# A four-layer transformer block and a three-branch block on one core: two-head attention groups, traded operand pairs, and a mixer tail in another order

## The chip, the cores and the metric

One core of a Trainium2 chip runs the whole program. The metric is the device time of one execution in microseconds; the page also gives the span, from the first to the last instruction of the core. A matmul runs on TensorE (PE), its weight load is listed as PEld; VectorE is DVE, ScalarE is ACT, GpSimd is POOL and the queue engine is SP.

## What is computed

T = 256 tokens of width 1024 pass through four layers and then a second block. A layer is: half a feed-forward, a mixer, half a feed-forward, and a gated addition of a projected per-layer embedding (the phase called `ple`):

```python
for layer in range(DEPTH):                    # 4
    h = x + 0.5 * swiglu(rmsnorm(x, g[0]), w_ffn_gu[layer, 0], w_ffn_down[layer, 0])
    h = h + mixer(rmsnorm(h, g[1]))           # hgrn2, mlstm, sliding window, hgrn2
    h = h + 0.5 * swiglu(rmsnorm(h, g[2]), w_ffn_gu[layer, 1], w_ffn_down[layer, 1])
    gate = jax.nn.sigmoid(rmsnorm(h, g[3]) @ w_ple_gate[layer])
    x = h + gate * (p[layer] @ w_ple_proj[layer])
```

The hgrn2 mixer ends with a norm per head, a gate and a projection:

```python
    o = rmsnorm(from_chunks(o), g_norm)
    o = o.reshape(B, T, D_MODEL).astype(x.dtype) * jax.nn.silu(og)
    return o @ w_out
```

The second block has three branches: dilated window attention (three groups of 8 heads of width 64, strides 1, 4 and 16, mixed by a softmax over their log-denominators, which is the same as one softmax over all three groups' masked scores), grouped attention with rotary positions (8 heads of 64, 2 key heads), and attention to 256 memory tokens (4 heads of 128). Each branch is gated by a silu and projected, the three are merged by sigmoid gates, projected once more, normalised and added to x. All inputs and outputs are float32.

## The kernel before

Activations lie feature-major in SBUF, as 8 chunks of 128 features by 256 tokens. Every weight matrix is cut into 407 **units** of 1 MB (128 partitions by 2048 numbers). A unit n passes through four engines:

- SP loads it into one of 4 slots of `raw`, as soon as unit n-4 has been split.
- ACT (`high`, L1127) rounds it to the 32-bit matmul type: `w_hi` = cast(raw), into one of 3 slots, once PE has used unit n-3.
- DVE (`low`, L1526) takes the rest: `w_lo` = raw - w_hi. It counts up `weights_split`.
- PE multiplies it: 48 matmuls of 128x128 by 128x256, three for each product of a block (`act_hi` by `w_hi`, `act_hi` by `w_lo`, `act_lo` by `w_hi`). `project` (L641) does 8 chunks k of a column unit, `project_tokens` (L656) the same with tokens on the partitions, `rows` (L670) a row unit into four accumulating banks.

Activations are split in the same way: `xg_hi`/`xg_lo` hold the normalised input of a phase without the norm's factor, and `mo_hi`/`mo_lo` the middle operand (hidden values of the feed-forward, the mixer's output, the embedding p in slots 4 and 5). DVE writes `xg` for the next phase in `next_operand` (two chunks: two TENSOR_SCALAR at L1568, then two SCALAR_TENSOR_TENSOR at L1571) and counts `x_updated` and `xg_ready`; the next phase's first `project` waits for `xg_ready` chunk by chunk. The norm's factor follows behind: ACT squares x (L1132), DVE adds the 8 chunks of squares (a TENSOR_REDUCE over a strided view, L1540), PE sums over partitions by a matmul with ones (`norm_sums`, L688; in the second block L685), ACT takes the logarithm and the exponential (L1138, L1141) into `rstd`, and DVE multiplies it into each PSUM bank as it is read (`scale`, L1577). Each engine has one instruction stream written out by hand. No scheduler reorders it, so what stands ahead on an engine is waited for.

The phases that the change touches:

- **ple** (units n0 to n0+4): PE does `rows(n0)` on p, then four `project`s of the gate weights, with `norm_sums` behind the first. DVE scales bank u, ACT takes its sigmoid (L1186), and DVE (`gated(u)`, L1648 and L1649) multiplies and adds to chunks 2u and 2u+1 of x. `xg` is still read by the last `project`, so the first `next_operand` waits for `weights_used` n0+5, which is that project's end.
- **hg** (hgrn2 mixer, layers 0 and 3): while PE does the projections n0+14 and n0+15, it also makes the outputs of the heads (L802 to L804) into banks 4 to 7 and the sums of their squares (`both_sums`, L813) into banks 2 and 3. ACT takes logarithms (L1247) and exponentials (L1253) of two pairs at a time. DVE normalises (L1812) and multiplies the gate (L1815); ACT casts (`operand`, L1257), DVE subtracts (`low_part`, L1819), and the output projection `w_out` starts as the pairs come (`mo_ready`).
- **second**: the memory operand is made during the last ple, with its own square sum on DVE (L1665). PE then does two memory projections, waits for the two norms (L1023, L685, L1028), and goes on. The attention runs in three stages, between the projections of other units: 9 units with the memory and grouped attention (6 **wide** groups of 4 slots by 256 keys, one in flight), 9 units with the first four dilated heads of each group (8 **narrow** groups: one head, 128 queries, 512 masked keys, two in flight), and 6 gate units with the last four heads (8 narrow groups, two in a unit). In each unit PE does: `project`, `rotate` (L1063, for the rotary products, stages one and two), `values(u-1)` (L931), `turn(u)` (transposes, L920), `scores(u+1)` (L910). DVE does: `scale`, `rope` (L2133 to L2136), `take(u-1)` (L1989), `logits(u+1)` (mask L1967, maximum L1969, bias L1970), `low`, `probs(u+1)` (L1978, L1981). ACT does:

```python
                    exps(0)
                    for u in range(9):
                        copies(u)
                        exps(u + 1)
                        high(n0 + 10 + 9 * half + u + SPLIT)
```

where `exps` (L1335) waits for the bias and `copies` (L1344) for the transposes.

## Time and profile before

| | |
|---|---|
| three runs | 2711.62, 2709.26, 2704.3 us, median 2709.26 us |
| the profiled execution | 2703.97 us |
| its span | 2702.2 us, mean granted TensorE clock 0.990 |
| PE | 2602.0 us busy (96%), 21152 matmuls |
| DVE | 1766.9 us (65%) |
| ACT | 1211.0 us (45%) |
| DMA | 435.51 MB, queue of the weights busy 44.3% |
| chain that ended last | PE 80%, DVE 13%, ACT 5%, issue 2% |

The matmuls overlap in the array: each is listed with about 283 ns, while one starts every 0.12 us. So the count times 0.12 us tells how long a unit keeps PE, 48 of them 5.76 us, and a unit that lasts longer has waited. An idle time is listed with what ended it.

### The profile page before, as it was taken

The page shows a single profiled execution, that of the slowest core. Times are in us where ns is not written, and L with a number is a line of the kernel's source. Part 1 is how long each engine was busy: PE and PEld are TensorE (multiplying, and loading weights), DVE is VectorE, ACT ScalarE, POOL GpSimd, SP SyncE. Part 2 cuts the span into 40 slices and gives each one's busy share as a digit, 9 for nine tenths or more (in the row PEclk, how much of TensorE's full clock was granted, in tenths as well). Part 3 has the DMA queues.
Part 4 walks back from the last instruction along what each step waited for, and adds up shares of the span by engine and source line. Part 5 has one row for each costly group of instructions (what it writes and reads, how often), then busy time and mean ns, then how long its engine had stood idle before and what let it go on. Part 6 is the DMA issues. An engine that isn't in the chain of part 4 may idle for free.

```text
span 2702.2 us, 49646 instructions
## 1 busy us (share of the span) xinstructions
PE 2602.0 (96%) x21152; PEld 2543.3 (94%) x21152; DVE 1766.9 (65%) x2230; ACT 1211.0 (45%) x1279; POOL 5.2 (0%) x13
## 2 busy tenths in 40 slices
PE   8999999999999999999969999999999999999997
PEld 8999999999998999999959999999999998888897
DVE  6558675586565755865676558656856568666665
ACT  4444354444444544444464335434354445433543
POOL 0000000000000000000000000000000000000000
PEclk9999999999999999999999999999999999999999
DMA  7554245445542455455424544544435544333351
GB/s 268 182 186 172 79 157 191 186 156 188 187 171 98 177 198 183 160 187 182 164 93 140 189 177 156 192 180 156 156 107 195 187 171 156 125 125 111 109 181 69
DMA packets 60193, 435.51 MB, mean 161 GB/s; under 512 B 6720, under 2 KB 6848, under 8 KB 7552
## 3 DMA queue, kind: packets, MB, share of 16 engines
q1 hardware_dynamic: 59184, 429.05, 44.3%
q0 software_dynamic: 848, 4.06, 0.4%
q8 instruction: 131, 2.15, 0.3%
q14 instruction: 30, 0.25, 0.0%
HBM read 432.04 MB, written 1.05 MB: 160 GB/s over the span
## 4 chain that ended last, share of the span: by engine, by line
PE 80%; DVE 13%; ACT 5%; issue 2%; DMA 0%; ACTq 0%; DVEq 0%
PE ps L641 52%; PE ps L670 19%; PE ps L656 4%; DVE w_lo L1526 4%; ACT w_hi L1127 3%; PE ps L780 2%; DVE xg_lo L1571 1%; DVE xg_hi L1568 1%; DVE scratch L1577 1%; DVE x L1633 1%; DVE tiny L1969 0%; PE ps L910 0%; DVE scratch L1981 0%; ACT scratch L1335 0%; DVE scratch L2085 0%
## 5 line engine op out<-in xcount | busy, mean ns | idle before, releaser
L1526 DVE TENSOR_TENSOR w_lo<-raw,w_hi 128x2048 fp32r<-128x2048 f32 x407 | 932.2, 2291 | 544.6 <-ACT w_hi L1127 544.3
L641 PE MATMUL ps<-xg_hi,w_hi 128*128 128x256 f32 x4240 | 1211.7, 286 | 27.7 <-DVE xg_lo L1571 24.8
L641 PE MATMUL ps<-xg_hi,w_lo 128*128 128x256 f32 x4240 | 1200.4, 283 | 0.0
L641 PE MATMUL ps<-xg_lo,w_hi 128*128 128x256 f32 x4240 | 1200.2, 283 | 0.0
L1127 ACT CAST w_hi<-raw 128x2048 fp32r<-128x2048 f32 x407 | 771.5, 1896 | 475.1 <-PE ps L670 250.9
L641 PEld LDWEIGHTS ps<-xg_hi,w_hi 128*128 128x128 f32 x4240 | 813.9, 192 | 37.8 <-issue 20.7
L641 PEld LDWEIGHTS ps<-xg_hi,w_lo 128*128 128x128 f32 x4240 | 814.2, 192 | 1.1 <-issue 0.5
L641 PEld LDWEIGHTS ps<-xg_lo,w_hi 128*128 128x128 f32 x4240 | 814.1, 192 | 0.0
L670 PE MATMUL ps<-mo_hi,w_hi 128*128 128x256 f32 x1568 | 445.0, 284 | 4.8 <-DVE xg_hi L1568 3.6
L670 PE MATMUL ps<-mo_hi,w_lo 128*128 128x256 f32 x1568 | 443.7, 283 | 0.0
L670 PE MATMUL ps<-mo_lo,w_hi 128*128 128x256 f32 x1568 | 443.7, 283 | 0.0
L1156 ACT ACTIVATE scratch<-scratch 128x256 f32<-128x256 f32 x176 | 73.7, 419 | 582.9 <-DVE scratch L1598 582.8
L670 PEld LDWEIGHTS ps<-mo_hi,w_hi 128*128 128x128 f32 x1568 | 300.9, 192 | 7.4 <-DVE xg_hi L1568 6.1
L670 PEld LDWEIGHTS ps<-mo_hi,w_lo 128*128 128x128 f32 x1568 | 301.0, 192 | 0.0
L670 PEld LDWEIGHTS ps<-mo_lo,w_hi 128*128 128x128 f32 x1568 | 301.0, 192 | 0.0
L1598 DVE TENSOR_TENSOR scratch<-ps,rstd 128x256 f32<-128x256 f32 x176 | 74.5, 423 | 145.8 <-PE ps L641 126.3
L641 PE MATMUL ps<-mo_hi,w_hi 128*128 128x256 f32 x352 | 102.5, 291 | 11.8 <-DVE mo_lo L1819 8.9
L641 PE MATMUL ps<-mo_hi,w_lo 128*128 128x256 f32 x352 | 101.3, 288 | 0.0
L641 PE MATMUL ps<-mo_lo,w_hi 128*128 128x256 f32 x352 | 101.2, 287 | 0.0
L1602 DVE TENSOR_TENSOR scratch<-scratch 128x256 f32<-128x256 f32 x176 | 75.2, 427 | 37.6 <-ACT scratch L1156 37.1
L656 PE MATMUL ps<-w_hi,xg_hi 128*128 128x256 f32 x320 | 91.7, 287 | 0.0
L656 PE MATMUL ps<-w_hi,xg_lo 128*128 128x256 f32 x320 | 90.6, 283 | 0.0
(273 smaller groups left out, 2175.2 us busy)
## 6 DMA issues: line engine op xcount, KB each, us to landing
raw<-weights_dram SPq DMA_DIRECT2D x407, 1024.0 KB, 4.8
x<-x_t_dram SPq DMA_DIRECT2D x1, 1024.0 KB, 7.7
scratch<-c_second_dram POOLq DMA_DIRECT2D x1, 1024.0 KB, 12.1
scratch<-p_t_dram POOLq DMA_DIRECT2D x4, 256.0 KB, 3.8
scratch<-mem_t_dram POOLq DMA_DIRECT2D x1, 1024.0 KB, 7.6
out_dram<-x SPq DMA_DIRECT2D x2, 512.0 KB, 2.6
common<-c_common_dram POOLq DMA_DIRECT2D x1, 640.0 KB, 9.1
smalls<-smalls_dram SPq DMA_DIRECT2D x1, 152.0 KB, 4.9
```

Source lines behind the costliest of these rows:

```text
L641: last = nc.tensor.matmul(bank(e, ring)[:, half * T:(half + 1) * T], l, r, start=(k == 0 and j == 0 and half == 0), stop=(k == KC - 1 and ...
L656: last = nc.tensor.matmul(bank(e, ring)[:, b * T:(b + 1) * T], l, r, start=(k == 0 and j == 0), stop=(k == KC - 1 and j == 2))
L670: last = nc.tensor.matmul(ps[:, 4 + c // 2, (c % 2) * T:(c % 2 + 1) * T], l, r, start=(first and k == 0 and j == 0 and c % 2 == 0), stop=( ...
L780: last = nc.tensor.matmul(o, HG_SUFFIX[:, at_:at_ + keys], upper(HG_PQ[:, at_:at_ + P], w), start=True, stop=True)
L1127: nc.scalar.copy(w_hi[:, m % SPLIT, :], raw[:, m % RAW, :]).then_inc(weights_hi, 1)
L1156: nc.scalar.activation(FFN_T[:, 2 + j % 2], FFN_T[:, j % 2], ACT.Silu).then_inc(silu_ready, 1)
L1526: V.tensor_tensor(w_lo[:, m % SPLIT, :], raw[:, m % RAW, :], w_hi[:, m % SPLIT, :].bitcast(F32), ALU.subtract).then_inc(weights_split, 1)
L1568: V.tensor_scalar(xg_hi[:, c], x[:, c], gain(g, c), None, ALU.mult).then_inc(x_updated, 1)
L1571: V.scalar_tensor_tensor(xg_lo[:, c], x[:, c], gain(g, c), xg_hi[:, c].bitcast(F32), ALU.mult, ALU.subtract).then_inc(xg_ready, 1)
L1577: V.tensor_tensor(dst, pair(e % ring, True), row(rstd[:], 2), ALU.mult).then_inc(bank_read, 1)
L1598: V.tensor_tensor(FFN_T[:, j % 2], pair(e)[:, 0], rstd[:], ALU.mult).then_inc(up_scaled, 1)
L1602: V.tensor_tensor(FFN_H[:, j % 2], FFN_T[:, 2 + j % 2], FFN_T[:, 4 + j % 2], ALU.mult).then_inc(hidden_value, 1)
```

## The change

It has seven parts.

1. **Trading pairs.** The two operand pairs are now called `left` and `right`, and `operands(i)` says which is xg and which mo in phase i: they trade places behind each of the first three ple phases. In ple, the next input is then written to the pair that is free, so the wait for `weights_used` n0+5 goes and `next_operand` moves ahead: two chunks at u = 1, 2 and 3 each, the last two behind `gated(3)`. At u = 3 ACT takes the sigmoid first and casts the weights second. The phase before the second block doesn't trade, but its memory operand moves by one u.
2. **Square sums.** `sum_chunks` replaces the TENSOR_REDUCE of all 17 norms and of the memory: three TENSOR_TENSOR adds, of 1024, 512 and 256 columns, each waiting for the one before.
3. **norm_sums in ple** is issued inside the first `project`, ahead of its chunk 4, and no longer behind it.
4. **The tail of hg.** ACT takes four logarithms, then four exponentials; the cast of unit n0+17 moves from between them to behind `operand(2)`. DVE scales gate 2 ahead of the first normalisation, and takes the low part of unit n0+17 last. PE makes the second half of the sums two chunks earlier.
5. **Two-head groups.** A dilated group now holds two heads (2 slots by 512 keys), with both heads' matmuls alternating; there are 4 groups in a stage and one in flight, in the same buffers and banks as the wide groups. Group u belongs to unit u, so the later units of a stage have none.
6. **values** of every group go through blocks first and heads second.
7. **Weights first.** In all three stages ACT's `high` stands ahead of `copies` and `exps` of the unit; in the third stage DVE's `low` stands ahead of `logits`.

```diff
+        def operands(i):
+            trades = min(sum(k == "ple" for k, _ in phases[:i]), DEPTH - 1)
+            return (right, left) if trades % 2 else (left, right)
...
-            for h in range(4):
+            for hp in range(2):
                 for n in range(TB):
-                    r = head_half(h)
-                    g = dict(slots=1, width=512, k0=0, scale=HD ** -0.5, scores=[], values=[], h=h, n=n)
+                    g = dict(slots=2, width=512, k0=0, scale=HD ** -0.5, scores=[], values=[], masked=True, hp=hp, n=n)
                     own_block = slice(n * P, (n + 1) * P)
                     for a, col, keys in ((0, 0, slice(0, T)), (1, 256, own_block), (2, 384, own_block)):
-                        c = 2 * a + h // 2
-                        g["scores"].append((col, keys.stop - keys.start, QA[r, c, own_block], KA[r, c, keys]))
+                        for h in range(2):
+                            r, c = head_half(h), 2 * a + hp
+                            g["scores"].append((512 * h + col, keys.stop - keys.start, QA[r, c, own_block], KA[r, c, keys]))
...
-                project(n0 + 1, e0, XG, (xg_ready, x0))
-                norm_sums(i)
+                project(n0 + 1, e0, XG, (xg_ready, x0), besides={4: lambda: norm_sums(i)})
...
-                project(n0 + 15, e0 + 15, XG, ring=2, besides={2: lambda: both_sums(2)})
+                project(n0 + 15, e0 + 15, XG, ring=2, besides={0: lambda: both_sums(2)})
...
-                    for r, col, vs in groups[g]["values"]:
-                        for j, (v, block_) in enumerate(vs):
+                    heads = groups[g]["values"]
+                    blocks = len(heads[0][2])
+                    for j in range(blocks):
+                        for r, col, vs in heads:
+                            v, block_ = vs[j]
...
-                roots(0)
-                high(n0 + 14 + SPLIT)
-                roots(2)
-                gate(2)
+                roots()
                 operand(0)
                 operand(1)
+                gate(2)
                 gate(3)
                 operand(2)
+                high(n0 + 14 + SPLIT)
                 operand(3)
...
                     for u in range(9):
+                        high(n0 + 10 + 9 * half + u + SPLIT)
                         copies(u)
                         exps(u + 1)
-                        high(n0 + 10 + 9 * half + u + SPLIT)
...
+            def sum_chunks(v, out):
+                link(V.tensor_tensor(v[:, 0:4], v[:, 0:4], v[:, 4:8], ALU.add))
+                link(V.tensor_tensor(v[:, 0:2], v[:, 0:2], v[:, 2:4], ALU.add))
+                return V.tensor_tensor(out, v[:, 0], v[:, 1], ALU.add)
...
-                V.tensor_reduce(SQ_SUM, SQ.rearrange("p c t -> p t c"), AX_X, ALU.add).then_inc(square_sum, 1)
+                sum_chunks(SQ, SQ_SUM).then_inc(square_sum, 1)
...
                 for u in range(4):
-                    if u == 3:
-                        gated(2)
-                        dve.wait_ge(weights_used, n0 + 5)
-                        if not to_second:
-                            next_operand(i, 0, 2)
                     scale(n0 + 1 + u, e0 + u, PLE_T[:, 2 * u:2 * u + 2])
-                    if u in (1, 2):
-                        gated(u - 1)
-                    if u < 2 or (u == 2 and to_second):
+                    if u and not to_second:
+                        next_operand(i, 2 * (u - 1), 2)
+                    if 0 < u < 3 and to_second:
+                        memory_operand(i, 2 + 2 * u, 2)
+                    if u < 3:
                         low(n0 + 1 + u + SPLIT)
+                    gated(u)
...
                 for u in range(6):
                     scale(n0 + 28 + u, e0 + 28 + u, t, ring=2)
-                    for g in (2 * u, 2 * u + 1):
-                        take(g - 2)
-                        logits(g + 2)
+                    take(u - 1)
+                    low(n0 + 28 + u + SPLIT)
+                    logits(u + 1)
                     dve.wait_ge(m["gate"], u + 1)
                     V.tensor_tensor(SE_O[:, c:c + 2], SE_O[:, c:c + 2], t, ALU.mult).then_inc(m["gated"], 1)
-                    low(n0 + 28 + u + SPLIT)
-                    probs(2 * u + 2)
-                    probs(2 * u + 3)
+                    probs(u + 1)
```

**DVE at the end of the first ple.** L1526 (now L1504) is `low`, L1577 (L1563) `scale`, L1648 and L1649 (L1634, L1635) `gated`, L1568 and L1571 (L1554, L1557) `next_operand`. Before, from u = 2 on:

```order
L1577 TENSOR_TENSOR scratch<-ps,rstd 128x512
L1648 TENSOR_TENSOR scratch<-scratch,ps 128x512
L1649 TENSOR_TENSOR x<-x,scratch 128x512
L1648 TENSOR_TENSOR scratch<-scratch,ps 128x512
L1649 TENSOR_TENSOR x<-x,scratch 128x512
L1568 TENSOR_SCALAR xg_hi<-x,smalls 128x256 x2
L1571 SCALAR_TENSOR_TENSOR xg_lo<-x,smalls,xg_hi 128x256 x2
L1577 TENSOR_TENSOR scratch<-ps,rstd 128x512
L1568 TENSOR_SCALAR xg_hi<-x,smalls 128x256 x2
L1571 SCALAR_TENSOR_TENSOR xg_lo<-x,smalls,xg_hi 128x256 x2
```

Now, from u = 2 on:

```order
L1563 TENSOR_TENSOR scratch<-ps,rstd 128x512
L1554 TENSOR_SCALAR right_hi<-x,smalls 128x256 x2
L1557 SCALAR_TENSOR_TENSOR right_lo<-x,smalls,right_hi 128x256 x2
L1504 TENSOR_TENSOR w_lo<-raw,w_hi 128x2048
L1634 TENSOR_TENSOR scratch<-scratch,ps 128x512
L1635 TENSOR_TENSOR x<-x,scratch 128x512
L1563 TENSOR_TENSOR scratch<-ps,rstd 128x512
L1554 TENSOR_SCALAR right_hi<-x,smalls 128x256 x2
L1557 SCALAR_TENSOR_TENSOR right_lo<-x,smalls,right_hi 128x256 x2
L1634 TENSOR_TENSOR scratch<-scratch,ps 128x512
L1635 TENSOR_TENSOR x<-x,scratch 128x512
```

The first operand chunks now stand ahead of the last `scale` by a whole unit; only chunks 6 and 7 stay behind the last `gated`.

**ACT at the tail of the first hg.** L1247 (now L1231) is the logarithm, L1253 (L1237) the exponential, L1242 (L1226) the silu of a gate, L1257 (L1241) the operand's cast, L1127 (L1108) `high`. Before:

```order
L1247 ACT_TABLE_LOAD
L1247 ACTIVATE scratch<-ps,eps 128x512 x2
L1253 ACT_TABLE_LOAD
L1253 ACTIVATE scratch<-scratch 128x512 x2
L1127 CAST w_hi<-raw 128x2048
L1247 ACT_TABLE_LOAD
L1247 ACTIVATE scratch<-ps,eps 128x512 x2
L1253 ACT_TABLE_LOAD
L1253 ACTIVATE scratch<-scratch 128x512 x2
L1242 ACT_TABLE_LOAD
L1242 ACTIVATE scratch<-scratch 128x512
L1257 CAST mo_hi<-scratch 128x512 x2
```

Now:

```order
L1231 ACT_TABLE_LOAD
L1231 ACTIVATE scratch<-ps,eps 128x512 x4
L1237 ACT_TABLE_LOAD
L1237 ACTIVATE scratch<-scratch 128x512 x4
L1241 CAST right_hi<-scratch 128x512 x2
L1226 ACT_TABLE_LOAD
L1226 ACTIVATE scratch<-scratch 128x512 x2
L1241 CAST right_hi<-scratch 128x512
L1108 CAST w_hi<-raw 128x2048
L1241 CAST right_hi<-scratch 128x512
```

Two table loads, one cast of weights and one silu are gone from ahead of the first operand casts.

**ACT in the second attention stage**, where L1335 (now L1315) is `exps` and L1344 (L1324) `copies`. Before, a stretch of three units:

```order
L1335 ACTIVATE scratch,tiny<-scratch,tiny 128x512
L1127 CAST w_hi<-raw 128x2048
L1344 COPY scratch<-ps 128x512
L1335 ACTIVATE scratch,tiny<-scratch,tiny 128x512
L1127 CAST w_hi<-raw 128x2048
L1344 COPY scratch<-ps 128x512
```

Now:

```order
L1315 ACTIVATE scratch,tiny<-scratch,tiny 128x512 x2
L1108 CAST w_hi<-raw 128x2048
L1324 COPY scratch<-ps 128x1024
L1315 ACTIVATE scratch,tiny<-scratch,tiny 128x512 x2
L1108 CAST w_hi<-raw 128x2048
L1324 COPY scratch<-ps 128x1024
```

The rows follow one another alike, but the cast now belongs to the unit of the copy behind it, not to the unit of the exponentials ahead of it. In unit u it waits only for that unit's `project`.

## Rows read from the trace of the kernel before

**Rows 1.** The page, part 1: busy time of each engine.
```profile
PE 2602.0 (96%) x21152; PEld 2543.3 (94%) x21152; DVE 1766.9 (65%) x2230; ACT 1211.0 (45%) x1279; POOL 5.2 (0%) x13
```
**Rows 2.** Waits of PE: us in total, times, longest us.
```profile
PE ps L641 <- DVE xg_lo L1571: 24.8, 26, 12.3
...
PE ps L920 <- DVE scratch L1981: 10.2, 13, 1.8
PE ps L641 <- DVE mo_lo L1819: 8.9, 2, 4.4
PE ps L685 <- DVE scratch L1540: 5.4, 1, 5.4
...
PE ps L931 <- DVE scratch L1989: 2.4, 2, 2.0
```
**Rows 3.** The chain from the first ple to its feed-forward: start us, us, what.
```profile
572.98 17.27 PE ps L641 x144
...
596.98 0.79 DVE xg_lo L1571 x2
...
600.03 6.01 PE ps L641 x48
```
**Rows 4.** Groups by line, whole span: busy us, mean ns, idle before.
```profile
L1526 DVE TENSOR_TENSOR w_lo<-raw,w_hi 128x2048 fp32r<-128x2048 f32 x407 | 932.2, 2291 | 544.6 <-ACT w_hi L1127 544.3
...
L1540 DVE TENSOR_REDUCE scratch<-scratch 128x256 f32<-128x2048 f32 x17 | 65.3, 3841 | 1.0 <-ACT scratch L1132 1.0
L1577 DVE TENSOR_TENSOR scratch<-ps,rstd 128x512 f32<-128x512 f32 x89 | 61.0, 687 | 31.9 <-PE ps L641 23.1 <-ACT rstd L1141 8.5
```
**Rows 5.** The chain from the start of `w_out` in the first hg.
```profile
343.88 36.50 PE ps L641 x288
```
**Rows 6.** The chain at the entry of the second block.
```profile
2266.71 1.28 ACT L1421
...
2271.27 7.95 PE ps L656 x48
```
**Rows 7.** Stretches: us, PE busy (matmuls), granted clock, DMA share, GB/s.
```profile
343.90:347.20 3.30, 3.30 (x15) 0.50 0.00 0
2265.30:2275.30 10.00, 6.29 (x25) 0.51 0.62 211
2324.40:2411.56 87.16, 80.76 (x639) 1.00 0.30 105
2411.56:2493.84 82.28, 79.30 (x581) 1.00 0.32 115
2493.84:2556.25 62.41, 57.91 (x442) 1.00 0.33 116
```
**Rows 8.** The chain through one unit of the first attention stage.
```profile
2364.46 2.29 DVE w_lo L1526
...
2374.18 1.80 ACT w_hi L1127
...
2376.00 2.29 DVE w_lo L1526
```
**Rows 9.** PE in time: a wide group's scores and values, a unit with a narrow group.
```profile
2357.28 1.13 PE L910 MATMUL ps<-scratch 64*128 64x256 f32 x8
...
2365.16 1.15 PE L931 MATMUL ps<-scratch 128*64 128x128 f32 x16
...
2436.53 0.59 PE L1063 MATMUL ps<-scratch,common 128*128 128x512 f32 x1
2437.05 1.09 PE L931 MATMUL ps<-scratch 128*64 128x128 f32 x8
2438.07 0.66 PE L920 MATMUL ps<-common,scratch 128*128 128x128 f32 x4
...
2438.66 1.14 PE L910 MATMUL ps<-scratch 64*128 64x256 f32 x6
```
**Rows 10.** Groups by form in the three stages (2324 to 2557 us).
```profile
L1969 DVE TENSOR_REDUCE tiny<-ps 128x4 f32<-128x1024 f32 x6 | 7.3, 1218 | 2.0 <-PE ps L910 1.9
```

174 lines of the change are left out of this document (78 added, 96 removed).

## The prediction

> **What bounds the kernel now.** The page's busy times come first: PE is busy for 96% of the span, DVE for 65%, ACT for 45% [rows 1]. A full unit keeps PE for 5.76 us (144 matmuls in 17.27 us, three units [rows 3]) and 407 of them make 2344 us. The count of projections doesn't change. So the change can give back only what PE waits for, and the 358 us in which it does other work. The waits of PE [rows 2] name the places: the next phase's input (24.8 us over 26 waits), the probabilities of the attention (10.2), the operand at the tail of hg (8.9, two tails), one square sum at the entry of the second block (5.4). The chain of waits then shows what each consists of, and the stretches [rows 7] show the three attention stages: 87.2, 82.3 and 62.4 us, in which PE is busy for 94% by the records. That busy time is no floor: part of it is matmuls that could run two at a time.
>
> A measurement of this kernel can tell about 0.3% (8 us) from no change.
>
> **Hand-over from ple to the next feed-forward (three times).** Before, PE leaves ple at 590.25 (572.98 + 17.27) and starts the second unit of the feed-forward at 600.03 [rows 3]: 9.78 us for a unit of 5.76. The second unit takes 6.01 instead of 5.76, so 4.3 us are lost; another 0.2 goes at its norm. DVE wrote all eight input chunks in that gap, the last low part at 596.98. Now six chunks are written ahead. Two stay behind the last `scale`. I follow DVE from PE's end T: `scale` until T+0.85, chunks 4 and 5 for 1.4 (two at 0.27 to 0.35 and two at 0.4 to 0.48, by that row of 0.79 for two), `gated(3)` for 1.45 (two of 0.69 as in [rows 4], and hand-offs), chunk 6 high and low for 1.1: T+4.85. PE gets to chunk 6 at T+4.3, so it waits for 0.55. All of DVE's work in a unit is 0.6+1.4+2.2+1.4 = 5.6 us against 5.76, just enough. The cost is at the start: the square sum (next part) is ready 1.0 us after PE gets to chunk 4 of the first `project`, which before it had finished without a wait. Gain: 4.5 - 0.55 - 1.0 = 2.95 us, **8.8** for three.
>
> **Square sums (18 times).** The reduce takes 3.84 us, the subtraction of 2048 columns 2.29 and the product of 512 columns 0.69 [rows 4]. That makes about 1.15 us for 1024 columns and 0.4 for 256, so three linked adds take 2.3 to 2.5 us: 1.4 saved each time. Most sums lie beside `project`s and gain nothing. At the entry of the second block two of them and the memory's lie in DVE's chain, which is full there: x is ready 2.5 us earlier, and ACT's chain behind it (table loads of 1.28 from 2266.71 on [rows 6]) releases PE 2.4 us earlier. There PE stood idle for about 7 us, the granted clock was 0.51 for the 10 us around it [rows 7], and a unit took 7.95 us where 5.95 is usual there [rows 6]. With 3.3 us idle, in two pieces, I expect full clock: 2.4 more. (In the third stage PE stood for 2.0 us in one piece [rows 2], at a granted clock of 1.00 [rows 7].) Taken: **4.8**; bounds 2.4 (clock as before) and 4.8.
>
> **Tail of hg (twice).** Before, PE ends its projections at 339.3 and starts `w_out` at 343.88; the 288 matmuls from there take 36.50 us for 34.56 [rows 5], as the clock was granted at 0.50 for 3.3 us [rows 7]. Loss: 4.5 + 1.9 = 6.4. Now the second pair of logarithms starts at 332.5 (sums made earlier), the only table load for exponentials ends at 335.3, four exponentials at 337.6; the first low part is written by 339.45 and PE waits for 0.3. Behind it stand three short waits: 1.25 (pair 2 needs the silu of gate 2, whose table load of 1.28 now comes later), 0.9 (pair 3 stands behind the moved cast of 1.9), 0.8 (the low part of unit n0+17, 2.29 [rows 4], now last on DVE). Gain: 6.4 - 3.25 = 3.1, **6.2** for two. If all three waits stay out it is 12; if the clock falls all the same, 2.
>
> **First attention stage.** Its chain is a closed circle through both engines [rows 8]: low part at 2364.46, probabilities, scale, rotary products, maximum, exponentials, weight cast (2374.18), low part at 2376.00. That is 11.5 us a unit. PE has only 9.9 us of work: 5.86 for the projection, 0.95 for the rotary product (two matmuls of 0.59, overlapped [rows 9]), and 1.0, 1.0 and 1.06 for values, transposes and scores. With the cast at the start of the unit, 1.9 + 1.6 us of ACT leave the circle and PE bounds it: five units win 0, 1.2, 1.9, 1.6 and 1.4 us: **6.1**. The memory groups' values span all 128 columns and win nothing.
>
> **Second stage.** A narrow group costs PE, from start to start [rows 9], 1.02 (values) + 0.59 (transposes) + 1.07 (scores) = 2.7 us, eight of them 21.4. The wide groups tell what two heads cost: their scores alternate between the halves of the array and 1024 key columns take 1.13 us, where a narrow group's 512 take 1.14; 16 instructions of values take 1.15, a narrow group's 8 take 1.09 [rows 9]. So both heads together cost one head's time: 1.0 + 1.0 + 1.07 = 3.1 us, four groups 12.4. Gain 9.0. PE's waits for probabilities behind the first group, 2.3, go too; DVE's pace (second rival) takes 0.4. Against it stands the stage's first group: with 1024 columns the mask add takes 1.3 and the maximum 1.22 [rows 10], exponentials 1.55, multiplies 0.9. It starts behind a low part, as before, and is ready 9.75 us after the stage's start where PE is ready after 7.0: 2.8 us idle, before 0.6. In all **8.7** of 82.3 us [rows 7].
>
> **Third stage.** The same: 9.0, and 3.8 us of waits and restarts gone (2.4 of them at L931 [rows 2]), less 2.2 at the first group: **10.6** of 62.4 us. Its units are tight. The probabilities are ready 9.6 us after the end of a `project`, and PE wants them after 10.0.
>
> **Sum.** 8.8 + 4.8 + 6.2 + 6.1 + 8.7 + 10.6 = 45.2 us. The profiled execution took 2703.97, so 2658.8. The median of the three runs is 5.3 above it: **2664 us**.
>
> **The skill against the trace.** Two heads at once cost what one does, by the rows above. The Trainium skill (TensorEngine Tiling (Array Packing), Performance Considerations) says that packing speeds up TensorE, not the reading of PSUM, and that the copy out may become the bottleneck. If so, DVE would pace the units, which is the second rival.
>
> **Rivals.**
> - *The heads don't overlap.* Each two-head group then costs 5.2 us instead of 3.1, eight of them 17: 2681. For it: the dilated heads mix blocks of 256 and 128 columns. Against it: [rows 9], with the same halves and banks. 0.10.
> - *DVE paces the attention.* In the second stage DVE has 2.5 (scale, rotary) + 0.3 + 2.7 + 2.3 + 1.1 = 8.9 us in a unit, and waits about 1.2 for the scores, which start 3 us behind the project: 10.1 against PE's 9.9. If the mask add, whose mask is read twice by a repeated row, or the order brings ACT's 1.6 into this circle, a unit takes 11.7: 14 us more, 2678. 0.13.
> - *The hand-over moves, and is not shortened.* DVE's 5.6 of 5.76 us in ple leaves nothing; if it falls behind by 3 us at u = 3, chunks 6 and 7 come as late as chunk 0 did. The 8.8 are gone: 2673. 0.07.
> - *One group in flight is too few (slower).* Place: `turn(u+1)` in stages two and three. Maximum, low part, exponentials and probabilities (2.75 + 2.3 + 1.6 + 1.05 = 7.7 us) end 1.8 us (second stage) or 0.4 us (third) ahead of PE. Where they end later, each us is PE's, once a group; if `project` covered none of them, 8 x 7.7 = 62 us: 2726. It decides from about 6.7 us late a group (54 us in all). 0.03, as the first stage works in this way already and PE waited there for 1.8 us at most.
> - *No effect*: the matmuls hide everything, 2709. 0.02. The waits in [rows 2] speak against it.
>
> **Numbers.** The forecast has 0.65. Its own uncertainty: without the three waits in each hg, the 2.8 us at two stage starts and the wait at chunk 4, 14 us less and with a quiet median 2648; with half of the attention's gain, 2677. The range takes in the first three rivals, two of them partly together: 2646 to 2688. Faster is the forecast and the first three rivals, 0.95; same 0.02; slower 0.03.
>
> **What would show it.** Right: PE's wait on the input chunks falls from 24.8 to about 14, of which 0.5 us is at each hand-over; a new wait of 1 us a ple on the square sum (inside the project); tails of hg with waits under 1.5 us and full clock; stages of about 81, 73.5 and 52 us; scores of a two-head group at 12 instructions in 1.2 us and values at 16 in 1.15; two waits of 2.8 us at the stages' starts. Wrong: scores and values of a group over 2 us each (first rival), units of 11 us and more with DVE busy throughout (second), over 3 us at the hand-over (third), waits at every transposition (fourth).

## The result, and the profile after

The changed kernel takes 2664.13 us (median of 4 runs, 2663.5 to 2664.88), the kernel before 2707.75 on the same chip: a ratio of 0.9844, 95% interval 0.9831 to 0.9856. The profiled execution took 2663.52 us, its span is 2661.7 (2702.2 before). The forecast was 2664. Three executions in these comparisons (two of the kernel before, beside experiments 4, 5 and 11, and one of experiment 12) took 6.4 to 11.2 ms and stand outside every figure.

The page, part 1, of the changed kernel:

```profile
PE 2582.1 (97%) x21152; PEld 2529.1 (95%) x21152; DVE 1733.4 (65%) x2226; ACT 1206.2 (45%) x1267; POOL 5.2 (0%) x13
```

PE issues as many matmuls as before and is busy for 20 us less [rows 1]: 15.6 of them in stages two and three (137.21 to 121.64, below), where pairs of matmuls that lay one behind the other now lie beside each other, the rest elsewhere. The other 20 us of the 40.5 are idle time. The waits of PE over the whole span (us in total, times, longest us):

```profile
PE ps L943 <- DVE scratch L2016: 15.9, 8, 5.1
PE ps L629 <- DVE left_lo L1557: 15.2, 10, 12.3
PE ps L900 <- DVE scratch L1967: 5.8, 3, 2.6
PE ps L676 <- DVE scratch L1519: 4.4, 4, 1.1
PE ps L629 <- DVE right_lo L1557: 3.1, 10, 0.4
...
PE ps L629 <- DVE right_lo L1800: 2.2, 3, 1.0
PE ps L629 <- DVE left_lo L1800: 2.2, 3, 1.0
```

Against [rows 2]: the input chunks fell from 24.8 to 18.3 (the two rows of L1557; 12.3 of either is the one wait at the start of the kernel, so the forecast's "about 14" asked for more than the hand-overs had, 2.4 us each by this list), the operand of the hg tails from 8.9 to 4.4 (L1800), the probabilities from 10.2 to 5.8 (L900). New is L676: 1.1 us in each of the four ple, for the square sum. The sliding window's L943 isn't touched by the change. Gone is one wait that the forecast doesn't name, in the second hgrn2 mixer of the kernel before, for the square sum behind its second unit:

```profile
PE ps L688 <- DVE scratch L1540: 1.4, 1, 1.4
```

One table holds all versions that ran. Each number is the time from the first matmul of the stretch's first unit to that of the next stretch, in the profiled executions. *Hand-over* is ple and the three units behind it (mean of three), *entry* the fourth ple and the second block's first ten units, *hg* a whole mixer, *rest* all other phases together. In the rest the versions run the same matmuls; what differs is 124.6 to 126.3 us in the mlstm mixer, 119.1 to 122.9 in the sliding window mixer and 145.9 to 147.4 in the second block's tail.

```
                        hand-over  entry    hg (two)       stage 1  2      3      rest
before                  53.06      106.43   163.61 165.79  85.86    84.18  59.44  1865.4
after                   50.39      103.34   160.86 161.19  79.41    74.63  52.27  1866.6
trade undone            54.18      103.34   160.85 161.17  79.42    74.61  52.29  1868.0
reduction again         53.18      108.95   160.85 162.55  79.42    74.59  50.71  1870.9
ones behind project     50.54      104.06   160.87 161.19  79.42    74.69  52.31  1867.8
trade alone there       50.54      105.77   160.87 162.55  79.42    74.69  52.29  1867.1
before + adds           52.86      104.78   163.58 163.89  85.86    84.17  60.78  1866.4
hg tail as before       50.39      103.36   163.55 164.45  79.41    74.61  52.28  1865.8
heads one by one        50.39      103.36   160.85 161.16  80.12    79.72  53.85  1868.0
weights cast last       50.40      103.37   160.85 161.19  85.82    80.35  61.77  1868.1
before + cast first     53.05      106.65   163.75 166.16  79.59    81.28  59.36  1870.9
first groups early      50.39      103.37   160.86 161.20  79.51    70.23  48.59  1865.0
 + ones at 6, hg cast   49.09      103.51   161.98 162.30  79.50    70.23  48.59  1865.9
 + ones at 5            49.66      103.86   160.84 161.20  79.50    70.23  48.60  1868.4
```

From before to after: hand-overs 3 x 2.67 = 8.0, entry 3.1, hg 2.75 + 4.6, stages 6.45 + 9.55 + 7.17, rest -1.2. That is 40.4 of the 40.5 us.

The chain of waits through the first hand-over after the change (start us, us, what):

```profile
563.88 2.21 DVE w_lo L1504
566.08 1.14 DVE scratch L1517
...
567.25 0.70 DVE scratch L1518
...
567.98 0.44 DVE scratch L1519
...
568.55 0.67 PE ps L676 x2
569.22 20.16 PE ps L629 x168
...
589.47 0.69 DVE scratch L1563
...
590.69 0.79 DVE right_lo L1557 x2
...
593.90 7.45 PE ps L629 x60
```

It goes as forecast: three adds of 1.14, 0.70 and 0.44 us, PE released by them inside the projection, 168 matmuls in one piece, and then only the last `scale`, chunks 4 and 5, the last residual and the high part and first low part of chunks 6 and 7 until 593.9, 4.5 us behind PE's end (T+4.85 in the forecast).

One unit of the second stage in the chain of waits:

```profile
2405.69 0.86 PE ps L1045 x2
2406.55 1.02 PE ps L914 x16
2407.58 1.02 PE ps L900 x8
2408.60 1.08 PE ps L891 x12
2409.68 5.93 PE ps L629 x48
```

In the stage's units behind the first group the chain is PE's alone: rotary product, values, transposes, scores, projection, 9.92 us a unit with no link through DVE or ACT. The forecast's 9.9 us a unit and its price of a two-head group (1.02 + 1.02 + 1.08 = 3.1 us) stand here link by link.

What did not go as forecast is the stages' first group. PE in time at the start of the second stage (start us, us, what, idle before it):

```profile
2393.11 0.28 PE L629 MATMUL ps<-right_lo,w_hi 128*128 128x256 f32 x1
2396.01 1.49 PE L900 MATMUL ps<-common,scratch 128*128 128x128 f32 x8 [2.62 <-DVE scratch L1967]
2397.43 2.08 PE L891 MATMUL ps<-scratch 64*128 64x256 f32 x12
```

2.9 us pass from start to start, as forecast (2.8), but the transposes then take 1.49 and the scores 2.08 us; of the usual unit in the chain above they took 1.02 and 1.08. Stretches of the changed kernel say why (us, PE, PEld, DVE, ACT and POOL busy, granted clock, DMA share, GB/s):

```profile
2248.60:2256.60 8.00, 5.72 (x27) 4.65 (x27) 7.97 (x12) 7.88 (x10) 0.00 (x0) 0.79 0.66 248
...
2386.31:2514.28 127.97, 121.64 (x1021) 112.07 (x1021) 92.16 (x116) 62.94 (x70) 0.00 (x0) 0.97 0.36 130
2396.00:2401.00 5.00, 4.99 (x31) 4.26 (x32) 1.96 (x3) 1.64 (x2) 0.00 (x0) 0.66 0.00 0
2470.60:2475.60 5.00, 4.96 (x31) 4.39 (x32) 4.66 (x4) 4.76 (x5) 0.00 (x0) 0.66 0.14 31
2624.30:2629.30 5.00, 4.99 (x29) 4.99 (x30) 2.89 (x2) 2.04 (x3) 0.00 (x0) 0.66 0.00 0
```

and of the kernel before, stages two and three, and the same place as the last row:

```profile
2411.56:2556.25 144.69, 137.21 (x1022) 123.01 (x1021) 98.79 (x156) 63.22 (x78) 0.00 (x0) 1.00 0.32 115
2666.20:2671.20 5.00, 4.96 (x41) 4.96 (x42) 2.89 (x2) 2.04 (x3) 0.00 (x0) 1.00 0.00 0
```

After each of the two idle gaps (2.6 us idle by the list of waits, 2.9 from start to start) the clock was granted at 0.66 over 5 us, about 3.4 of them at the lower level (1.2 GHz in place of 2.4). It fell a third time, behind a wait of 2.1 us from start to start in the second block's tail that both kernels have and that the kernel before came through at 1.00; the tail is 1.5 us longer for it, 147.4 us for 145.9.

### The profile page after: what moved, and what is told of

It is laid out like the page before. It is cut to its first block, busy times and chain, and to the rows that moved or that the text cites. A ratio compares the mean times of both kernels' runs of the same rounds, so it can differ in the third digit from the quotient of the medians.

```text
span 2661.7 us, 49606 instructions
## 1 busy us (share of the span) xinstructions
PE 2582.1 (97%) x21152; PEld 2529.1 (95%) x21152; DVE 1733.4 (65%) x2226; ACT 1206.2 (45%) x1267; POOL 5.2 (0%) x13
## 4 chain that ended last, share of the span: by engine, by line
PE 85%; DVE 10%; ACT 4%; issue 1%; DMA 0%; ACTq 0%; DVEq 0%
PE ps L629 55%; PE ps L658 19%; PE ps L644 5%; DVE w_lo L1504 2%; ACT w_hi L1108 2%; PE ps L767 2%; DVE x L1619 1%; PE ps L891 1%; DVE scratch L1563 1%; DVE right_lo L1557 1%; PE ps L900 1%; PE ps L914 1%; DVE left_lo L1557 1%; DVE right_hi L1554 0%; DVE left_hi L1554 0%
## 5 line engine op out<-in xcount | busy, mean ns | idle before, releaser
L1504 DVE TENSOR_TENSOR w_lo<-raw,w_hi 128x2048 fp32r<-128x2048 f32 x407 | 932.2, 2291 | 505.6 <-ACT w_hi L1108 505.5
L1108 ACT CAST w_hi<-raw 128x2048 fp32r<-128x2048 f32 x407 | 771.6, 1897 | 525.8 <-PE ps L658 251.3
L629 PE MATMUL ps<-right_hi,w_hi 128*128 128x256 f32 x2544 | 727.0, 286 | 7.1 <-DVE right_lo L1557 3.1
L629 PE MATMUL ps<-right_hi,w_lo 128*128 128x256 f32 x2544 | 720.1, 283 | 0.0
L629 PE MATMUL ps<-right_lo,w_hi 128*128 128x256 f32 x2544 | 719.9, 283 | 0.0
L629 PE MATMUL ps<-left_hi,w_hi 128*128 128x256 f32 x2048 | 586.3, 286 | 19.7 <-DVE left_lo L1557 15.2
L629 PE MATMUL ps<-left_hi,w_lo 128*128 128x256 f32 x2048 | 581.2, 284 | 0.0
L629 PE MATMUL ps<-left_lo,w_hi 128*128 128x256 f32 x2048 | 581.1, 284 | 0.0
L629 PEld LDWEIGHTS ps<-right_hi,w_hi 128*128 128x128 f32 x2544 | 488.3, 192 | 13.9 <-issue 5.4
L629 PEld LDWEIGHTS ps<-right_hi,w_lo 128*128 128x128 f32 x2544 | 488.5, 192 | 0.6 <-issue 0.2
L629 PEld LDWEIGHTS ps<-right_lo,w_hi 128*128 128x128 f32 x2544 | 488.3, 192 | 0.0
L629 PEld LDWEIGHTS ps<-left_lo,w_hi 128*128 128x128 f32 x2048 | 394.8, 193 | 0.0
L658 PE MATMUL ps<-left_hi,w_hi 128*128 128x256 f32 x832 | 236.1, 284 | 2.9 <-DVE right_hi L1554 1.8
L658 PE MATMUL ps<-left_hi,w_lo 128*128 128x256 f32 x832 | 235.4, 283 | 0.0
L658 PE MATMUL ps<-left_lo,w_hi 128*128 128x256 f32 x832 | 235.4, 283 | 0.0
L658 PE MATMUL ps<-right_hi,w_hi 128*128 128x256 f32 x736 | 208.9, 284 | 1.8 <-DVE left_hi L1554 1.8
L658 PE MATMUL ps<-right_hi,w_lo 128*128 128x256 f32 x736 | 208.3, 283 | 0.0
L658 PE MATMUL ps<-right_lo,w_hi 128*128 128x256 f32 x736 | 208.3, 283 | 0.0
L1584 DVE TENSOR_TENSOR scratch<-ps,rstd 128x256 f32<-128x256 f32 x176 | 74.5, 423 | 156.1 <-PE ps L629 126.3
```

The source lines that it names most:

```text
L629: last = nc.tensor.matmul(bank(e, ring)[:, half * T:(half + 1) * T], l, r, start=(k == 0 and j == 0 and half == 0), stop=(k == KC - 1 and ...
L658: last = nc.tensor.matmul(ps[:, 4 + c // 2, (c % 2) * T:(c % 2 + 1) * T], l, r, start=(first and k == 0 and j == 0 and c % 2 == 0), stop=( ...
L1108: nc.scalar.copy(w_hi[:, m % SPLIT, :], raw[:, m % RAW, :]).then_inc(weights_hi, 1)
L1504: V.tensor_tensor(w_lo[:, m % SPLIT, :], raw[:, m % RAW, :], w_hi[:, m % SPLIT, :].bitcast(F32), ALU.subtract).then_inc(weights_split, 1)
L1584: V.tensor_tensor(FFN_T[:, j % 2], pair(e)[:, 0], rstd[:], ALU.mult).then_inc(up_scaled, 1)
```

## The experiments

Each kernel was timed against the kernel before on one chip; the table above has the stretches of each. 

**1. The trade of pairs undone.**

```diff
-            return (right, left) if trades % 2 else (left, right)
+            return (left, right)
...
+                    if u == 3:
+                        gated(2)
+                        dve.wait_ge(weights_used, n0 + 5)
+                        next_operand(i, 0, 2)
...
+                    next_operand(i, 2, 4)
```

> The changed kernel with one part undone: the operand pairs trade places no more at the three ple phases, and the order of gates, scalings, input chunks and weight casts there is that of the kernel before. My theory: the wait for the first half of the hand-over's operands ends on two of the four scalings only because the first chunks go to the pair that no matmul reads any more; so each of the three hand-overs grows by the 3 to 4 us that the input-chunk wait had shrunk by, less what the norm sums at chunk 4 keep: about 2.7 us each, +8 us in all, 2672 us, all of it in the three stretches from ple to the first projections of the next ffn. Rival: the transfer of the chunks was hidden by the norm factor anyway, and then the time stays at 2664 and the three stretches keep their length.

Measured: 2676.3 us, ratio 0.9896 (0.9879 to 0.9912). Each hand-over is 3.8 us longer, 11.4 in all, where 8 were expected; everything else keeps its length but the rest, which takes 1.4 more. The hand-over is even 1.1 us longer than in the kernel before, although square sums and ones-matmuls are the new ones. (ACT's new order at u = 3 stays too.) DVE in time behind PE's last ple projection (start us, us, what):

```profile
589.21 0.61 DVE L1554 TENSOR_SCALAR left_hi<-x,smalls 128x256 fp32r<-128x256 f32 x2 [1.82 <-PE ps L629]
...
596.53 4.49 DVE L1504 TENSOR_TENSOR w_lo<-raw,w_hi 128x2048 fp32r<-128x2048 f32 x2
```

All eight chunks and a weight's low part stand behind the projection again. So the whole gain of the hand-over hangs on the trade: the other two parts without it cost 1.1 us.

**2. The strided reductions again.**

```diff
-                sum_chunks(SQ, SQ_SUM).then_inc(square_sum, 1)
+                V.tensor_reduce(SQ_SUM, SQ.rearrange("p c t -> p t c"), AX_X, ALU.add).then_inc(square_sum, 1)
```

(and the same for the memory's squares)

> The changed kernel with one part undone: the two sums of squares over the eight chunks are one strided reduction each again, not three adds. My theory: at each of the three ple phases that hand over to an ffn, and at the entry to the second block, the ones-matmuls of the squares wait for this sum, so each of these waits grows by the 1.5 us between the reduction (3.8 us) and the three adds (2.3 us): +4.5 us in the ple phases and +3 us or more at the entry, where two such sums follow each other; 2672 us. Rival: in the ple phases the wait at chunk 4 only moves a wait that comes later anyway (the norm factor), so only the entry pays: +3 us, 2667 us.

Measured: 2679.4 us, ratio 0.9905 (0.9889 to 0.9922), 7 us more than expected. Each ple is 2.8 us longer, not 1.4, and the entry 5.6 us, of which 2.8 lie in its ple. The stretches of this kernel around the wait:

```profile
566.00:570.00 4.00, 1.62 (x14) 1.45 (x13) 4.00 (x3) 2.18 (x2) 0.00 (x0) 1.00 0.70 231
570.00:574.00 4.00, 4.00 (x20) 3.95 (x21) 1.95 (x1) 2.18 (x3) 0.00 (x0) 0.57 0.24 61
```

PE waits 2.4 us in place of 1.1, and then its clock is granted at 0.57 for 4 us: 1.4 us of wait bring 1.4 us of clock. The price of a wait was right, that of the clock behind it was left out, as at the stages' starts. Two more places pay. The second hgrn2 mixer is 1.4 us longer, by the wait of 1.4 us on this sum that the kernel before has too. Of 4.3 us in the rest 1.6 lie in the mlstm mixer, where one wait is 2.1 us in place of 0.4 (the kernel before, with the same reduction, takes 124.7 there, so why it grew isn't shown), and 2.7 in the sliding window mixer. The third stage, against that, is 1.6 us shorter: PE waits 2.9 us at its start as in the changed kernel, but the clock behind stays up:

```profile
2490.20:2495.20 5.00, 4.95 (x44) 4.62 (x45) 4.86 (x4) 4.77 (x5) 0.00 (x0) 1.00 0.15 28
```


**3. The ones-matmuls behind the first projection again**, and **4. the same with the reductions**, so that only the trade is left of the hand-over's three parts.

```diff
-                project(n0 + 1, e0, XG, (xg_ready, x0), besides={4: lambda: norm_sums(i)})
+                project(n0 + 1, e0, XG, (xg_ready, x0))
+                norm_sums(i)
```

> The changed kernel with one part undone: in ple the ones-matmuls of the squares stand behind the first projection again, not at its chunk 4. My theory: the waits of 4.4, 4.0 and 1.1 us on the square sum (over the span) go, but the norm factor that the scalings of the hand-over wait for comes later by the four chunks, 1.5 to 2 us for each of the three; together 0 to 4 us more in the three hand-overs: 2664 to 2668 us. Rival: the chunks pace the hand-over and not the norm factor; then the waits' removal is all that is left, and the time falls by 2 to 3 us, to 2661 us.

The text reads the list's "4.4, 4, 1.1" as three waits; it is 4.4 us in 4 waits, the longest 1.1. Measured: 2666.1 us, ratio 0.9839 (0.9824 to 0.9854): no difference from the changed kernel that this measurement can tell. In the trace ple is 1.33 us shorter and what follows 1.49 longer. The chain of waits of this kernel has another path now:

```profile
570.24 0.47 ACT rstd L1120
...
572.45 1.80 ACT w_hi L1109
...
574.28 2.29 DVE w_lo L1505
...
579.93 2.20 DVE w_lo L1505
```

From the norm's factor on, a weight cast on ACT and then DVE's row of low parts and scalings set the end; PE's projections don't. With the matmuls at chunk 4 PE sets it, after an idle 1.3 us. Two paths of nearly the same length, so moving the matmuls wins nothing.

> The changed kernel with two parts undone together: the strided reductions are back, and the ones-matmuls of the squares stand behind ple's first projection again, so that of the hand-over's three parts only the trade of pairs is left. My theory: with the matmuls behind the projection the reduction is done in time, so the trade alone gives each hand-over its 2.5 us, within 0.3 us of the changed kernel's 50.4 us; the two other parts are worth nothing there, and only the entry pays the slower sums, 3 us: 2667 to 2669 us. Rival: the parts work together, and each hand-over without them is 1.3 us or more longer: 2671 us or above.

Measured: 2669.2 us, ratio 0.9862 (0.9846 to 0.9879). The hand-over takes 50.54 us, as in experiment 3. So the trade alone gives 2.5 of the 2.67 us; adds and chunk 4 together give 0.15. The entry is 2.4 us longer, where 3 were expected, and the second hgrn2 mixer 1.4, where nothing was.

**5. The kernel before with the adds alone.**

> The kernel before with the square sums as three adds alone. My theory: in ple the matmuls stand behind the projection and the sum is ready anyway, so the hand-overs keep their 53.1 us; the entry gains what the changed kernel gained there, 3 us: ratio to the kernel before 0.999. Rival: the 1.5 us shorter sum moves VectorE's whole row in ple forward, and each hand-over gets about 1.3 us shorter too: 7 us in all, ratio 0.9975.

Measured: ratio 0.9998 (0.9989 to 1.0008). The hand-over gains 0.2 us and the entry 1.65, half of what was expected: the rival is out, and the theory right in the hand-over and too high at the entry. The second hgrn2 mixer gains 1.9, which neither theory nor rival names: 1.35 in its second unit (6.35 us for 7.70), whose wait for the sum is gone, and 0.5 in the first unit of its `w_out` (7.53 for 8.03), which is clock. The third stage (+1.3) and the tail (+1.5) take 2.8 back, with the same waits of PE as before.

**6. The tail of hg as before.** The diff is the change's own part 4, turned round.

> The changed kernel with one part undone: the tail of hg as before (roots in two halves with a cast between them, normalise and gate by halves, both sums at chunk 2). My theory: the tail's two stretches grow back by what they lost between the two traces, 2.75 us and 4.6 us: +7.4 us, 2671 us, in the stretch from the last hg projection to the first w_out matmuls. Rival: part of what the stretch lost came from the trading of pairs or from the clock and not from the order of the tail; then it is +4 us or less, 2668 us.

Measured: 2668.7 us, ratio 0.9873 (0.9857 to 0.989). The two mixers grow by 2.7 and 3.3 us, 6.0 in all, between theory and rival. In the first mixer that is the whole difference to the kernel before. In the second, 1.3 of the 4.6 us remain, and they are the square sum's: the mixer's second unit takes 7.70 or 7.71 us in all four kernels with the reduction (before, experiments 2, 4 and 9) and 6.33 to 6.35 in the ten with the adds. So neither part 4 nor the clock makes this piece, but part 2.

**7. Heads one by one.**

```diff
-                    for a, col, keys in ((0, 0, slice(0, T)), (1, 256, own_block), (2, 384, own_block)):
-                        for h in range(2):
+                    for h in range(2):
+                        for a, col, keys in ((0, 0, slice(0, T)), (1, 256, own_block), (2, 384, own_block)):
...
-                    for j in range(blocks):
-                        for r, col, vs in heads:
+                    for r, col, vs in heads:
+                        for j in range(blocks):
```

> The changed kernel with the two heads of each group issued one after the other instead of in turn, for the scores of stages 2 and 3 and for the value matmuls of all stages. My theory: matmuls of the two heads use different rows or columns of the array and run side by side only where they are neighbours in the queue, so that 12 score matmuls of a dilated two-head group take about 2.1 us instead of 1.2 and the value matmuls of a group 2.1 instead of 1.15: about 0.9 to 1.9 us for each of the 16 groups of stages 2 and 3 and 0.9 for the 9 of stage 1, at most +30 us and, as in part the chain of a group hides behind the projections' matmuls, at least +10: 2674 to 2694 us. Rival: the queue lets them overlap however they stand, as the value matmuls of the wide groups of before did; then the value matmuls keep 1.15 us and only the scores lengthen, or nothing does: 2664 to 2672 us.

The text counts 16 groups in stages two and three and 9 in stage one; there are eight and six. Measured: 2671.6 us, ratio 0.9881 (0.9864 to 0.9897), stages +0.7, +5.1 and +1.6 (only the sum of the last two tells something, as the clock fell for longer in the second and not at all in the third). PE in time, first the changed kernel's second group, then this one's:

```profile
2406.49 1.09 PE L914 MATMUL ps<-scratch 128*64 128x128 f32 x16
...
2408.53 1.15 PE L891 MATMUL ps<-scratch 64*128 64x256 f32 x12
```

```profile
2410.20 1.58 PE L914 MATMUL ps<-scratch 128*64 128x128 f32 x16
...
2412.74 1.68 PE L891 MATMUL ps<-scratch 64*128 64x256 f32 x12
```

Values take 0.49 us more and scores 0.53. Eight groups at that price are 8.2 us, 6.7 were measured. By the time the rival is right (2664 to 2672), by the mechanism it lies between the two, since the values lengthen as well: issued head by head the matmuls still overlap in part (16 values one after the other would be near twice 1.09, [rows 9] has 8 in 1.09), and the alternation gives the other part.

**8. Weights cast last in the slots.**

```diff
-                        high(n0 + 10 + 9 * half + u + SPLIT)
                         copies(u)
                         exps(u + 1)
+                        high(n0 + 10 + 9 * half + u + SPLIT)
```

(in the third stage so for `high` on ACT and `low` on DVE)

> The changed kernel with one part undone: in the slots of the dilated attention ACT casts the weights last again, behind its copies and exponentials, and in stage 3 VectorE does so behind the logits and the gating. My theory: the next slot's projection waits for that cast, and in stage 2 and 3 the two-head groups put the longer work of a group in front of it; stage 1 grows back by its 6.4 us, stages 2 and 3 by 5 us each or more: 2680 us or above. Rival: with two-head groups the copies and exponentials of stages 2 and 3 are short enough, so that only stage 1 pays: 2670 us.

Measured: 2684.3 us, ratio 0.991 (0.9895 to 0.9925): the stages grow by 6.4, 5.7 and 9.5 us. The first is back at its old length, the third is 2.3 us over it; its clock, 1.00 in the kernel before [rows 7], is 0.92 here. The chain of waits in the second stage of this kernel:

```profile
2411.28 1.80 ACT w_hi L1108
...
2423.26 1.80 ACT w_hi L1108
...
2425.08 2.29 DVE w_lo L1504
...
2428.42 1.26 PE ps L900 x8
2429.68 2.03 PE ps L891 x12
...
2431.73 1.24 DVE scratch L1953
...
2435.97 1.80 ACT w_hi L1108
```

This is the circle of [rows 8] again, with a two-head group in it: 12.0 and then 12.7 us from cast to cast, where the changed kernel takes 9.92 a unit. The second round has a piece at half clock in it (0.50 from 2429.3 to 2432.5), so that its transposes and scores take 1.26 and 2.03 us, not 1.02 and 1.08.

**9. The kernel before with the cast first in stages one and two.**

> The kernel before with one thing of the change alone: ACT casts the weights first in the slots of stages 1 and 2, the dilated groups staying one head each in stage 2 and the four-head groups of stage 1 as they are. My theory: all of stage 1's gain (6.4 us) comes from this order, and stage 2 gains little of its 9.5 us, at most 2, since there the number of groups sets the pace: 2698 to 2701 us, measured beside the 2704.5 to 2707.8 of the kernel before. Rival: the order is what pays in stage 2 as well, and two-head groups alone are worth little: 2688 to 2691 us.

Measured: 2698.6 us, ratio 0.9963 (0.9951 to 0.9975): stage 1 is 6.3 us shorter, stage 2 2.9. With experiment 8 the second stage's 9.55 us come apart: order alone 2.9, two heads alone 3.8 (84.18 to 80.35), both 9.55. The parts are worth 2.8 us more together, of which about 1.2 are the piece at half clock in experiment 8. With the order alone PE waits for probabilities for 0.5 us in the whole second stage, and its own work on eight one-head groups sets the pace; with two heads alone the circle through ACT and DVE does. Each part takes away one of two limits.

**10. The first groups of stages two and three one slot early.**

```diff
+                        if u == 7:
+                            pe.wait_ge(m["roped"], 15 if half else 9)
+                            group_steps(att_before(i, 2 + half), dilated_groups(half))[0](0)
```

(the scores on PE; ACT's exponentials, DVE's logits and probabilities of that group move likewise)

> The changed kernel with the first group of stages 2 and 3 started one slot early: its scores, logits, exponentials and probabilities are issued in the last slot but one of the stage before, so that nothing stands idle where a stage begins. My theory: the two idle gaps of 2.9 us at the starts of stages 2 and 3 go, and with them the stretch at half clock behind each, worth about 1.7 us: 2 x 4.6 = 9 us, 2655 us. Rival: the slots at the end of a stage are full, and what the early group adds there shows as a wait of its copies or of the weights cast; then about half is given back, 2660 us.

Measured: 2655.5 us, ratio 0.9806 (0.9793 to 0.982). The stages lose 4.4 and 3.7 us, the tail 1.5. By the starts of the matmuls the two idle gaps had been 2.8 us each beyond the usual distance, 5.6 together. In the third stage a shorter wait is new, in the waits from 2380 to 2510 us:

```profile
PE ps L900 <- DVE scratch L1969: 0.7, 1, 0.7
```

That leaves 8.1 - 5.6 + 0.7 = 3.2 us for the clock behind the two gaps, 1.6 each. The stretch of the stage's first group, and the one in the tail behind its wait, which stands as before:

```profile
2387.50:2399.50 12.00, 12.00 (x105) 11.67 (x104) 8.01 (x9) 6.08 (x7) 0.00 (x0) 1.00 0.49 175
2614.00:2621.00 7.00, 5.24 (x44) 5.03 (x43) 4.43 (x5) 3.12 (x4) 0.00 (x0) 1.00 0.00 0
```

Both are at full clock, the second with PE idle for 1.8 of its 7 us. Experiment 2 agrees: one gap without the clock behind it made its stage 1.6 us shorter. The tail's 1.5 us are no work of the edit, its wait is the same. This version beats both kernels.

**11. That version with the ones-matmuls at chunk 6 and an earlier cast in hg**, and **12. with them at chunk 5 alone.**

```diff
-                project(n0 + 1, e0, XG, (xg_ready, x0), besides={4: lambda: norm_sums(i)})
+                project(n0 + 1, e0, XG, (xg_ready, x0), besides={6: lambda: norm_sums(i)})
...
-                operand(2)
                 high(n0 + 14 + SPLIT)
+                operand(2)
```

> The version with the early first groups, and beside it two shifts: in ple the ones-matmuls of the squares stand at chunk 6 of the first projection in place of chunk 4, and in the tail of hg ACT casts one weight piece before its third operand and not behind it. My theory: the sum of squares is ready 1.1 us after chunk 4 begins, and two chunks take 1.4 us, so at chunk 6 nothing stands idle for it while the norm factor comes as early as at chunk 4; since each hand-over then ends when its last projection ends, each gets 1.1 us shorter: 3.3 us over the three, and about 1 us at the entry. The cast in hg gives 0 to 2 us. Together 2650 us beside the 2655.5 of the version with early groups. Rival: VectorE's row of casts and scalings sets the end of the hand-over as it does where the sums stand behind the projection, and the 1.1 us comes back as a wait for the input chunks: no change, 2655 us.

Measured: 2654.0 us, ratio 0.9809 (0.9794 to 0.9824). The hand-overs lose 1.3 us each, as expected and against the rival; the entry loses nothing (its ple is 1.3 us shorter and the ten units behind it 1.5 longer, with the clock at 0.50 from 2249.6 to 2256.3, where the changed kernel has 0.77), and the earlier cast costs each mixer 1.1 us. Of 3.9 us gained 2.2 were given back there.

> The version with the early first groups, and beside it the ones-matmuls of the squares in ple at chunk 5 of the first projection; the tail of hg is that of the changed kernel. My theory: a chunk of this projection is 12 matmuls and 1.44 us, the sum of squares is ready as chunk 5 begins, and so TensorE's idle 1.3 us at chunk 4 goes without a later norm factor: each hand-over 49.1 us as with chunk 6 (50.4 before), the entry 1 us shorter too, hg without the 1.1 us that the earlier cast cost there twice: 2655.5 - 3.9 - 1.0 = 2650.6 us. Rival: the entry stays as long as it was with chunk 6, and the clock takes back 1 to 2 us elsewhere: 2652 to 2654 us.

Measured: 2655.6 us, ratio 0.9809 (0.9796 to 0.9822), against the theory and above the rival. At chunk 5 PE still waits 0.4 us for the sum, so a hand-over loses 0.7 us, not 1.3, and the entry is 0.5 us longer than with chunk 4. The rest took 3.3 us more than in experiment 10, all of it in the sliding window mixer. The mixer's last eight units in the changed kernel and in this one:

```profile
1339.70:1438.70 99.00, 76.62 (x605) 66.52 (x605) 69.24 (x167) 53.62 (x112) 0.00 (x0) 0.91 0.24 86
```

```profile
1337.70:1440.50 102.80, 81.02 (x605) 70.32 (x605) 69.37 (x167) 53.62 (x112) 0.00 (x0) 0.87 0.23 83
```

The same 605 matmuls, the same 53.62 us of ACT, a clock of 0.87 for 0.91: 3.8 us. Versions 10, 11 and 12 can't be told apart by time; the plain one, number 10, is the one to keep.

## Why the prediction was right, and where it was off

The total came out within a microsecond, and four of six terms within 1.2; but the sum itself was 4.8 us too large, 45.2 for 40.4. That the total still fits is luck: the forecast put 5.3 us between the profiled execution and the median, which were 0.6 this time (2663.52 and 2664.13), and the two errors cancel. A slip without consequence: the 358 us called other work are the span less the projections, waits included; PE's busy time leaves 2602 - 2344 = 258.

- **Hand-over, 8.8 forecast, 8.0 measured.** The chain is the forecast one. Sizes were a little off: the wait for chunk 6 was 0.2 us, not 0.55, that for the square sum cost PE 1.33, not 1.0. What the forecast did not see is that the adds and chunk 4, which it prepared the sum by, weren't needed there: the trade, with the order of DVE and ACT that it allows, gives 7.6 alone (experiment 4).
- **Entry, 4.8 forecast, 3.1 measured.** The entry's first ten units gained 4.4. The term left out that part 3 also stands in the fourth ple, whose new wait costs 1.33 there with no hand-over to win back from. The adds give 1.65 to 1.7 of the 3.1 (experiment 5, and experiment 4 against 3), where the forecast had 2.4 before the clock. The idle time fell to 3.2 us in two pieces (from start to start), as forecast; "full clock" was nearly right, 0.79 over 8 us in place of 0.51 over 10 [rows 7].
- **Tail of hg, 6.2 forecast, 7.35 measured**, of which experiment 6 shows 6.0 for the order. The surplus of 1.3 belongs to another term: "most sums lie beside `project`s and gain nothing" was wrong for one sum, that of the second hgrn2 mixer, where PE had waited 1.4 us for it. In the tail the three waits came where they were forecast, 1.0, 0.6 and 0.5 us long, behind a first one of 0.6. (Ahead of the first operand casts ACT is rid of three table loads, that of the silu included, and not of two.)
- **First stage, 6.1 forecast, 6.45 measured**; the cast's place alone gives 6.3 (experiment 9) and its return takes 6.4 (experiment 8).
- **Stages two and three, 8.7 + 10.6 forecast, 16.7 measured together** (144.69 to 127.97 us in the stretches). The units are as forecast. The missing 2.6 us are the step "2.8 us idle": it was priced as idle time alone. The clock behind the two gaps cost 3.2 (experiment 10), and 0.6 us were won elsewhere. The only row the forecast had on this, one wait of 2.0 us in the third stage at 1.00, which it used for the entry, doesn't carry over to these 2.9 us, nor, in the tail, to another wait of 2.1.
- **Not forecast:** the tail's +1.5 us, clock again, with the same wait as before.

The rivals: *the heads don't overlap* fell by the timeline, 12 scores in 1.15 us and 16 values in 1.09; its distance is what experiment 7 shows in part. *DVE paces the attention* fell by the chain, in which the second stage's units have PE links alone; so the rule that the Trainium skill gives (TensorEngine Tiling (Array Packing), Performance Considerations), that copying out of PSUM may become the bottleneck once TensorE packs its work, doesn't bind here. The Trainium skill says so there of a fourfold speed-up; here two heads share the array. Experiment 8 shows how near it is: with the cast last the same groups run at 12.0 to 12.7 us a unit, through DVE and ACT. *The hand-over moves* fell: 50.4 for 53.1 us. *One group in flight is too few* fell with it, PE waits for probabilities three times in all, 5.2 of the 5.8 us at the starts of stages two and three.

Left open: why the clock is granted in full behind one wait of 2.0 us and not behind another, or behind the gap of 2.9 us at the third stage in experiment 2 and not in the changed kernel; what part of the entry's gain the clock makes, which fell there for longer or shorter in versions that differ little; and how much of the entry is bound by ACT's chain; no run changed that chain by itself.

## What to carry to other kernels

Price an idle gap of the bound engine with what follows it: 2.8 us of idle PE cost 4.4 here, and 2.4 us in place of 1.1 cost 2.8 more. It is a risk and no fixed price: the gap at the third stage cost nothing beyond itself in experiment 2. Where two parts of a change loosen one circle, undo each alone and try each alone: the parts gave 2.9 and 3.8 us, both together 9.55, of which some is clock, so read the granted clock before calling the surplus an interaction; at the hand-over one part gave nearly all and the others nothing. And look at the first turn of a pipelined stage: its steps can often be issued in the stage before, which was worth as much here (8.1 us in the two stages) as the whole hand-over.

## What the runs showed of the hardware

- The granted clock makes differences in code that is the same. The same wait of about 2 us in the tail was followed by 1.00 in one kernel and 0.66 over 5 us in another, a gap of 2.9 us at the third stage by 0.66 in the changed kernel and 1.00 in experiment 2, and the last eight units of the sliding window mixer took 99.0 and 102.8 us with the same instructions, at mean clocks of 0.91 and 0.87. The rest of the kernel, where the versions run the same matmuls, scatters by 6 us between them, as much as several parts of this change are worth. A stretch by stretch table keeps them apart, a total doesn't.
- Matmuls on different column halves overlap even when each head's eight are issued one after the other: 16 in 1.58 us, 1.09 when they alternate.
- The reduction of 8 chunks of 256 over a strided view took 3.84 us [rows 4], three adds of halves 1.14 + 0.70 + 0.44 = 2.3 us in the chain.
